# First stage of a two-block transformer kernel: which conditioning blocks are loaded and summed before the tokens are normalised

## Chip, cores and metric

The kernel runs on one core of a Trainium2 chip. The metric is the device time of one execution in microseconds; the kernel before was run three times, and it was profiled in one further execution.

## What is computed

The reference runs two transformer-like blocks on 512 tokens of width 1024, in f32. The first block starts with a conditioning step (adaptive norm), and only that and the first projection matter here:

```
c_act = silu(c)                                  # 1024 values
mod = c_act @ ada_w + ada_b                      # 6 parts of 1024: sh_t, sc_t, g_t, sh_c, sc_c, g_c
h = rms_norm(x, tm_pre_g) * (1 + sc_t) + sh_t    # 512 x 1024
p = h @ w_in                                     # all branches of the token mixer start here
```

After that come a mixer with four branches, a feed-forward network, a second block with sparse attention, and a second feed-forward network. All of them use the weights once, as they stream in.

## The kernel before

**Layout.** Activations are held transposed: 1024 channels are 8 chunks `c` of 128 partitions, with the 512 tokens along the free axis. Every f32 matrix product is made of three matmuls on split operands (`h_hi`, `h_lo` and `w_hi`, `w_lo`; lines 1244 to 1246). A weight unit `u` is 128x2048 elements, 1 MB. ScalarE copies it to `w_hi` (`split(u)`, line 716), VectorE or GpSimd makes `w_lo` from it (`lo(u)`, line 1830 or 630), and then TensorE may use it (`weights_ready(u)`). Raw weights have two buffers.

**Conditioning.** `ada_w` is 1024 x 6144. It is loaded in blocks `n` of 1 MB, 256 columns each. Blocks 0 to 7 hold the shift (`sh_t`, blocks 0 to 3) and the scale (`sc_t`, blocks 4 to 7) of the first norm. Pair `j` is the blocks `j` and `4 + j`; it belongs to the channel chunks `2j` and `2j + 1`. VectorE and TensorE share its product with `c_act`: VectorE folds six of the eight row chunks into one (`ada_sum(j)`, one instruction of line 1871 and five of line 1873), TensorE takes the other two with 16 single-column matmuls (`ada_begun(j)`, line 1385) and then adds VectorE's result with 8 more, which sum over the partitions (`ada_ended(j)`, line 1393). `ada_pair(j)` on VectorE turns the result into the shift and the gain of two chunks, and `norm_pair(j)` makes the two chunks of `h`: VectorE scales (line 1900), ScalarE makes `h_hi` (`norm_hi`, line 751), VectorE makes `h_lo` (line 1905). The scaled chunks pass through `tbuf`, which has two slots, so a pair needs the slots of the pair before it.

**Tokens.** `x` comes as four DMAs of 0.5 MB (`x_tok`, 128 tokens each). ScalarE squares and sums them, and makes 1/rms for each token. VectorE puts these on diagonals (`x_diagonal`, line 1910), and one f32 product with a matrix of ones, `ss0` (line 1410), spreads them over the partitions. TensorE transposes `x` chunk by chunk (`x_turned`, line 1336, four transposes each); ScalarE copies the chunks out (`x_copied`).

**First unit.** The weight unit `sc` is multiplied as the chunks of `h` come: `first_unit(j)` is the 12 matmuls of chunks `2j` and `2j + 1` (two output tiles of three matmuls each). Every wait stands in the order of the engine's program, and nothing overtakes it. TensorE's order before is:

```
ada_begun(0), x_turned(0..3), ada_ended(0), ss0, x_turned(4..7), weights_ready(sc),
ada_begun(1), first_unit(0), ada_ended(1), ada_begun(2), ada_ended(2), ada_begun(3),
first_unit(1), ada_ended(3), first_unit(2), first_unit(3), turn_vectors(1..5), unit sc+1, ...
```

**Queues.** SP issues the loads in one order written out by hand: blocks 0 and 4, `x`, unit `sc`, blocks 1, 5, 2, 6, then (after the last transpose of `x`, whose space they take) 3 and 7, then the next weight units as their buffers come free. GpSimd issues the constants (`cst`, the first 128 KB and the other 868 KB separately) and the small vectors, ScalarE the vectors that are needed first. After the first unit VectorE makes `lo(sc+1)`, copies the turned vectors, and the kernel goes on unit by unit.

Of the kernel before, what the change touches and what calls it, by code (L numbers as in the profile page):

```python
# [27 lines left out]
EPS = 1e-6  # L28
# [122 lines left out]
def program(nc, A, out):  # L151
# [10 lines left out]
    with ctx:  # L162
# [5 lines left out]
        def sem(name):  # L168
            if name not in sems:
                sems[name] = ctx.enter_context(nc.semaphore(name))  # L170
            return sems[name]
# [47 lines left out]
        ada_pairs = [area(at, KT, 4 * P) for at in (4864, 4864 + 2 * UNIT, 4864 + 4 * UNIT, 0)]  # L219
# [19 lines left out]
        def vector_load(eng, g):  # L239
            r = 0  # L240
            for name, n in VECTORS[g]:
                base, _, tap = name.partition("/")
                a = A[base]
                if tap:
                    src = a[0, int(tap), :].rearrange("(t p) -> t p", p=P)
                elif len(a.shape) == 3:
                    src = a[0].rearrange("k (t p) -> (k t) p", p=P)
                else:
                    src = a[0].rearrange("(t p) -> t p", p=P)
                eng.dma_start(rows_in[r:r + n, g, :], src).then_inc(sem(f"vec_in{g}"), 16)  # L250
                r += n
# [30 lines left out]
        one = small[:, 249:250]  # L282
# [5 lines left out]
        fin_s, eps = small[:, 224:236], small[:, 255:256]  # L288
# [44 lines left out]
        U, unit = {}, 0  # L333
# [140 lines left out]
        def _(sp):  # L474
# [41 lines left out]

            w, w2 = A["w_in"][0], A["w_in_2"][0]

            for n in (0, 4):
                ada_load(sp, n)  # L520
            for tt in range(TT):
                sp.dma_start(x_tok[:, tt, :], A["x"][0, tt * P:(tt + 1) * P, :]).then_inc(sem(f"x_in{tt}"), 16)

            u = U["sc"]
            cols(u, w, KT, C_SC + MIX, MIX)
            for n in (1, 5, 2, 6, 3, 7):
                if n == 3:
                    wait_full(sp, T["xT"][KT - 1])
                ada_load(sp, n)
# [81 lines left out]
        def _(pool):  # L611
            pool.dma_start(cst[:, 0:2 * P], A["consts"][:, 0:2 * P]).then_inc(sem("consts_in"), 16)
            pool.dma_start(bias_if[:, 0:1], A["ml_i_bias"].rearrange("a h -> h a")).then_inc(sem("bias_in"), 16)
            pool.dma_start(bias_if[:, 1:2], A["ml_f_bias"].rearrange("a h -> h a")).then_inc(sem("bias_in"), 16)
            pool.dma_start(gl_low[:, S:S + MIX], A["gla_w_a2"][0]).then_inc(sem("bias_in"), 16)
            for g in range(2, len(VECTORS)):
                vector_load(pool, g)
            pool.dma_start(cst[:, 2 * P:], A["consts"][:, 2 * P:N_CONST]).then_inc(sem("consts_rest"), 16)
            pool.memset(eps, EPS).then_inc(sem("eps_set"), 1)
            pool.memset(one, 1.0).then_inc(sem("eps_set"), 1)  # L620

            wait_full(pool, T["vec"][-1])
            pool.wait_ge(sem("consts_rest"), 16)
# [20 lines left out]
            for n in range(MT * TT):  # L644
                t, j = divmod(n, TT)
# [60 lines left out]
        def _(act):  # L706
# [4 lines left out]
            def split(u, i=0, units=0):  # L711

                act.wait_ge(loaded[u % 2], loaded_at(u) + (i * 16 if units else 0))
                if u >= 2:
                    act.wait_ge(w_used, u - 1 + i)
                act.activation(w_hi[u % 2][:, :], raw[u % 2][:, :], ACT.Copy).then_inc(hi_done, 1)  # L716
# [29 lines left out]
            def norm_hi(shift=None, cs=range(KT)):  # L746
                for c in cs:
                    hn[0] += 1
                    act.wait_ge(sem("h_t"), hn[0])
                    b = 0.0 if shift is None else mod[:, shift + c:shift + c + 1]  # L750
                    act.activation(h_hi[:, c, :], tbuf[:, c % 2, :], ACT.Identity, bias=b).then_inc(sem("h_hi"), 1)
# [39 lines left out]
            def x_copied(cs):  # L791
                for c in cs:
                    t = T["xT"][c]
                    wait_full(act, t)
                    act.activation(x[:, c, :], bank[t.bank][:, :], ACT.Copy).then_inc(sem("x_ready"), 1)
                    act.wait_ge(sem("x_ready"), c + 1)
                    act.nop().then_inc(read[t.bank], 1)

            x_copied(range(3))
            split(0)  # L800
            t = T["ss0"][0]
            wait_full(act, t)
            release(act.activation(rstd[:, :], bank[t.bank][:, :], ACT.Copy, scale=float(D)), t)
            x_copied(range(3, 5))
            norm_hi(0, range(2))
            x_copied(range(5, KT))
            norm_hi(0, range(2, 6))
            u = U["sc"]
            split(u + 1)
            norm_hi(0, range(6, KT))  # L810
# [426 lines left out]
        def _(pe):  # L1237
# [138 lines left out]
            def ada_begun(j):  # L1376

                t = T["ada0"][j]
                wait_free(pe, t)
                pe.wait_ge(sem("c_act"), 1)  # L1380
                for n in (j, 4 + j):
                    pe.wait_ge(sem(f"ada_in{n}"), 16)
                for at, w in ada_columns_of(j):
                    for k in range(ADA_SUMMED, KT):
                        pe.matmul(bank[t.bank][:, at:at + 1], w[:, k, :], c_act[:, k:k + 1], start=at == 0 and k == ADA_SUMMED, stop=False,
                                  skip_group_check=True)

            def ada_ended(j):

                t = T["ada0"][j]  # L1390
                pe.wait_ge(sem("ada_summed"), j + 1)
                for at, w in ada_columns_of(j):
                    mm = pe.matmul(bank[t.bank][:, at:at + 1], w[:, 0, :], one, start=False, stop=True, skip_group_check=True)
                    if at % 2:
                        mm.then_inc(sem("ada_turned"), 1)

            def x_turned(cs):
                for c in cs:
                    turn(T["xT"][c], [(tt * P, x_tok[:, tt, c * P:(c + 1) * P]) for tt in range(TT)])

            ada_begun(0)
            for tt in range(TT):
                pe.wait_ge(sem(f"x_in{tt}"), 16)
            x_turned(range(4))
            pe.wait_ge(sem("eps_set"), 2)
            ada_ended(0)
            t = T["ss0"][0]
            wait_free(pe, t)
            pe.wait_ge(sem("x_diagonal"), 1)
# [3 lines left out]
            def first_unit(j):  # L1413
                fresh_units(u, T["sc"][0:2], (2 * j, 2 * j + 1), j == 0)

            ada_begun(1)
            first_unit(0)
            ada_ended(1)
            ada_begun(2)
            ada_ended(2)  # L1420
            ada_begun(3)
            first_unit(1)
            ada_ended(3)
            first_unit(2)
            first_unit(3)
# [398 lines left out]
        def _(dve):  # L1824
            ch = Chain(dve, "dve_step")

            def lo(u, i=0):

                dve.wait_ge(hi_done, u + 1 + i)
                dve.tensor_tensor(w_lo[u % 2][:, :], raw[u % 2][:, :], w_hi[u % 2][:, :].bitcast(FP32), ALU.subtract)\  # L1830
                   .then_inc(parted[u % 2], 1)
# [62 lines left out]
            def norm_pair(j):  # L1894
# [7 lines left out]
                for c in (2 * j, 2 * j + 1):  # L1902
# [2 lines left out]
                    dve.scalar_tensor_tensor(out=h_lo[:, c, :], in0=tbuf[:, c % 2, :], scalar=mod[:, c:c + 1],  # L1905
                                             in1=h_hi[:, c, :].bitcast(FP32), op0=ALU.add, op1=ALU.subtract).then_inc(sem("h_ready"), 1)

            ada_sum(0, ada_pairs[0])
            dve.wait_ge(sem("x_rms"), 1)
            dve.tensor_tensor(tbuf[:, 0, :].rearrange("p (a b) -> p a b", a=TT), ident.unsqueeze(1).broadcast_to([P, TT, P]),  # L1910
                              rstd_tok.unsqueeze(2).broadcast_to([P, TT, P]), ALU.mult).then_inc(sem("x_diagonal"), 1)
            lo(U["sc"])
            ada_pair(0)
            wait_read(dve, T["ss0"][0])
            norm_pair(0)
            for j in range(1, 4):
                ada_sum(j, ada_pairs[j])
                if j > 1:
                    ada_pair(j - 1)
                    norm_pair(j - 1)  # L1920
            ada_pair(3)
            norm_pair(3)
            dve.wait_ge(sem("consts_rest"), 16)
            lo(U["sc"] + 1)
            for g in range(1, len(VECTORS)):
# [260 lines left out]
            for c in range(MT):  # L2186
# [17 lines left out]
                for hh in range(2):  # L2204
                    n = 2 * c + hh
# [383 lines left out]
            for c in range(4):  # L2589
                for k in range(2):  # L2590
                    t = T["wo2"][2 * c + k]
                    wait_full(dve, t)
                    n = 2 * c + k
# [18 lines left out]
            for tt in range(TT):  # L2612
                n = 2 * tt
# [41 lines left out]
```

## Time and profile before

| what | value |
|---|---|
| median of three runs | 1675.08 us (1673.26 to 1675.53) |
| the profiled execution: its own time | 1675.9 us |
| its span (first to last instruction) | 1673.7 us |
| TensorE busy | 1615.5 us, 97% of the span |
| VectorE, ScalarE, GpSimd busy | 923.5, 611.2 and 239.4 us |
| mean granted TensorE clock | 0.984 of full |
| bytes moved by DMA | 170.42 MB, 102 GB/s on average |

All times below are microseconds from the span's start. A busy time of TensorE includes matmuls that overlap in its pipeline, so the distance between starts is the better measure of a matmul.

### The profile page before, as it was taken

How to read it: one execution, taken by the hardware profiler on the slowest of the kernel's cores; microseconds unless marked ns; L12 is line 12 of the kernel's file. 1: busy time of each engine (PE TensorE's matmuls, PEld its weight loads, DVE VectorE, ACT ScalarE, POOL GpSimd, SP SyncE). 2: the span in 40 equal slices, each digit the busy share in tenths (PEclk: the TensorE clock that was granted, in tenths of full speed). 3: DMA queues.
4: the chain of work that ended last, by engine and by line, in shares of the span. 5: the costliest groups of instructions: out<-in, count | busy, mean ns of one | idle time of the engine just before them, and what ended most of it. 6: DMA issues, size and time to landing. Idle time of an engine off the chain costs nothing.

```text
span 1673.7 us, 19853 instructions
## 1 busy us (share of the span) xinstructions
PE 1615.5 (97%) x7586; PEld 1305.4 (78%) x7586; DVE 923.5 (55%) x1262; ACT 611.2 (37%) x766; POOL 239.4 (14%) x132
## 2 busy tenths in 40 slices
PE   5999999989999799999999899999999999999998
PEld 5887678768888488888888687877788888888887
DVE  5559355428786644444433667766335655556333
ACT  4333353233234443333322532343543433334223
POOL 1210024120002011101000000334342111111000
PEclk9999999989999899999999999999999999999999
DMA  9233113206763123333222234222123333332221
GB/s 334 77 101 101 51 52 100 76 26 204 227 222 101 51 76 100 100 100 100 101 92 85 74 89 134 76 76 76 51 76 101 107 86 97 100 100 100 98 92 62
DMA packets 192226, 170.42 MB, mean 102 GB/s; under 512 B 9543, under 2 KB 180900, under 8 KB 192164
## 3 DMA queue, kind: packets, MB, share of 16 engines
q1 hardware_dynamic: 174240, 150.16, 29.4%
q10 hardware_dynamic: 16948, 16.89, 3.1%
q0 software_dynamic: 976, 2.52, 0.4%
q8 instruction: 42, 0.69, 0.2%
q14 instruction: 20, 0.16, 0.0%
HBM read 165.54 MB, written 2.10 MB: 100 GB/s over the span
## 4 chain that ended last, share of the span: by engine, by line
PE 89%; DVE 6%; ACT 2%; DMA 1%; issue 1%; SPq 0%; POOL 0%; DVEq 0%; ACTq 0%
PE bank L1244 24%; PE bank L1246 23%; PE bank L1245 23%; PE bank L1251 3%; PE bank L1253 3%; PE bank L1252 3%; DVE w_lo L1830 1%; DVE work L1968 1%; PE bank L1336 1%; PE bank L1773 1%; DMA work<-in_x 1%; PE bank L1558 1%; ACT w_hi L716 1%; PE bank L1348 1%; PE bank L1758 1%
## 5 line engine op out<-in xcount | busy, mean ns | idle before, releaser
L1244 PE MATMUL bank<-h_hi,w_hi 128*128 128x512 f32 x1536 | 611.8, 398 | 12.7 <-DVE h_lo L2349 5.4
L1246 PE MATMUL bank<-h_hi,w_lo 128*128 128x512 f32 x1536 | 601.9, 392 | 0.0
L1245 PE MATMUL bank<-h_lo,w_hi 128*128 128x512 f32 x1536 | 601.2, 391 | 0.0
L1830 DVE TENSOR_TENSOR w_lo<-w_raw,w_hi 128x2048 fp32r<-128x2048 f32 x102 | 234.5, 2299 | 259.1 <-ACT w_hi L716 258.8
L1244 PEld LDWEIGHTS bank<-h_hi,w_hi 128*128 128x128 f32 x1536 | 290.5, 189 | 95.7 <-issue 27.9
L716 ACT ACTIVATE w_hi<-w_raw 128x2048 fp32r<-128x2048 f32 x131 | 250.1, 1909 | 275.1 <-PE bank L1246 170.0
L1246 PEld LDWEIGHTS bank<-h_hi,w_lo 128*128 128x128 f32 x1536 | 290.2, 189 | 62.1
L1245 PEld LDWEIGHTS bank<-h_lo,w_hi 128*128 128x128 f32 x1536 | 290.7, 189 | 59.1 <-issue 1.0
L630 POOL TENSOR_TENSOR w_lo<-w_raw,w_hi 128x2048 fp32r<-128x2048 f32 x29 | 134.3, 4630 | 545.2 <-ACT w_hi L716 545.2
L1244 PE MATMUL bank<-y_hi,w_hi 128*128 128x512 f32 x304 | 121.4, 399 | 4.9 <-DVE work L2116 3.6
L667 POOL TENSOR_TENSOR work<-work 128x512 f32 x44 | 57.0, 1296 | 458.4 <-ACT work L1044 458.4
L1246 PE MATMUL bank<-y_hi,w_lo 128*128 128x512 f32 x304 | 119.3, 392 | 0.0
L1245 PE MATMUL bank<-y_lo,w_hi 128*128 128x512 f32 x304 | 119.1, 392 | 0.0
L2318 DVE SCALAR_TENSOR_TENSOR work<-bank,par,work 128x511 f32<-128x511 f32 (+1 forms) x88 | 61.5, 743 | 77.8 <-ACT work L1038 77.8
L1038 ACT ACTIVATE work<-work,par 128x512 f32<-128x512 f32 x44 | 35.8, 815 | 106.8 <-DVE work L2307 106.8
L1244 PEld LDWEIGHTS bank<-y_hi,w_hi 128*128 128x128 f32 x304 | 57.7, 190 | 19.7 <-DVE work L2116 4.0
L1873 DVE SCALAR_TENSOR_TENSOR work<-work,small 128x256 f32<-128x256 f32 (+1 forms) x132 | 69.3, 525 | 4.7
L1251 PE MATMUL bank<-w_hi,y_hi 128*128 128x512 f32 x176 | 69.2, 393 | 0.0
L1038 ACT ACTIVATE work<-bank,par 128x512 f32<-128x512 f32 x44 | 30.0, 686 | 107.3 <-PE bank L1246 107.2
L1253 PE MATMUL bank<-w_lo,y_hi 128*128 128x512 f32 x176 | 68.5, 389 | 0.0
L1252 PE MATMUL bank<-w_hi,y_lo 128*128 128x512 f32 x176 | 68.5, 389 | 0.0
L1246 PEld LDWEIGHTS bank<-y_hi,w_lo 128*128 128x128 f32 x304 | 57.6, 189 | 12.4
(280 smaller groups left out, 1608.6 us busy)
## 6 DMA issues: line engine op xcount, KB each, us to landing
w_raw<-in_w_in SPq DMA_DIRECT2D x94, 512.0 KB, 4.7
w_raw<-in_ffn_w_up SPq DMA_DIRECT2D x44, 512.0 KB, 4.7
w_raw<-in_w_up SPq DMA_DIRECT2D x44, 512.0 KB, 5.0
work<-in_ada_w ACTq DMA_DIRECT2D x16, 1024.0 KB, 7.5
w_raw<-in_ffn_w_down SPq DMA_DIRECT2D x22, 512.0 KB, 4.0
w_raw<-in_w_down SPq DMA_DIRECT2D x22, 512.0 KB, 3.8
work<-in_ada_w SPq DMA_DIRECT2D x8, 1024.0 KB, 11.5
w_raw<-in_w_o SPq DMA_DIRECT2D x8, 512.0 KB, 4.5
```

What stands on the lines that cost most here:

```text
L630: pool.tensor_tensor(w_lo[u % 2][:, :], raw[u % 2][:, :], w_hi[u % 2][:, :].bitcast(FP32), ALU.subtract)\
L716: act.activation(w_hi[u % 2][:, :], raw[u % 2][:, :], ACT.Copy).then_inc(hi_done, 1)
L1038: act.activation(cbuf[:, k, part, :], src, ACT.Identity, scale=par[:, bass.ds(i * 2 + at, 1)], **kw).then_inc(sem("center" + n), 1)
L1244: pe.matmul(dst, w_hi[s][:, at:at + n], hi, start=first, stop=False)
L1245: pe.matmul(dst, w_hi[s][:, at:at + n], lo, start=False, stop=False)
L1246: return pe.matmul(dst, w_lo[s][:, at:at + n], hi, start=False, stop=last)
L1251: pe.matmul(dst, hi, w_hi[s][:, at:at + n], start=first, stop=False, skip_group_check=onto)
L1252: pe.matmul(dst, lo, w_hi[s][:, at:at + n], start=False, stop=False, skip_group_check=onto)
L1253: return pe.matmul(dst, hi, w_lo[s][:, at:at + n], start=False, stop=last, skip_group_check=onto)
L1830: dve.tensor_tensor(w_lo[u % 2][:, :], raw[u % 2][:, :], w_hi[u % 2][:, :].bitcast(FP32), ALU.subtract)\
L1873: ins = dve.scalar_tensor_tensor(out=unit[:, 0, :], in0=unit[:, k, :], scalar=c_act[:, k:k + 1], in1=unit[:, 0, :], op0=ALU.mult, op1=ALU.add)
L2318: ins = dve.scalar_tensor_tensor(out=c[:, back:S], in0=src[:, 0:S - back], scalar=w, in1=c[:, back:S], op0=ALU.mult, op1=ALU.add)
```

## The change

SP loads two pairs (blocks 0, 4, 1, 5) ahead of `x` instead of one. GpSimd's load of the other constants (868 KB) waits until VectorE has made `x_diagonal`, and its two small memsets move ahead of the vector loads. VectorE sums pairs 0 and 1 and finishes both before it touches the tokens, then norms both, then makes `lo(sc)`, then sums pairs 2 and 3, and only then finishes and norms these two. TensorE opens and closes both first pairs before the transposes, and multiplies the first four chunks of unit `sc` in one piece of 24 matmuls, between `ada_begun(2)` and `ada_ended(2)`. ScalarE's `split(0)` moves from ahead of the norm to between its first and second pair.

```diff
-            for n in (0, 4):
+            for n in (0, 4, 1, 5):
                 ada_load(sp, n)
             for tt in range(TT):
                 sp.dma_start(x_tok[:, tt, :], ...)
             cols(u, w, KT, C_SC + MIX, MIX)
-            for n in (1, 5, 2, 6, 3, 7):
+            for n in (2, 6, 3, 7):
...
 (GpSimd)
+            pool.memset(eps, EPS).then_inc(sem("eps_set"), 1)
+            pool.memset(one, 1.0).then_inc(sem("eps_set"), 1)
             for g in range(2, len(VECTORS)):
                 vector_load(pool, g)
+            pool.wait_ge(sem("x_diagonal"), 1)
             pool.dma_start(cst[:, 2 * P:], A["consts"][:, 2 * P:N_CONST]).then_inc(sem("consts_rest"), 16)
-            pool.memset(eps, EPS).then_inc(sem("eps_set"), 1)
-            pool.memset(one, 1.0).then_inc(sem("eps_set"), 1)
...
 (ScalarE)
             x_copied(range(3))
-            split(0)
             (rstd from ss0)
             x_copied(range(3, 5))
             norm_hi(0, range(2))
+            split(0)
+            norm_hi(0, range(2, 4))
             x_copied(range(5, KT))
-            norm_hi(0, range(2, 6))
+            norm_hi(0, range(4, 6))
             split(u + 1)
             norm_hi(0, range(6, KT))
...
 (TensorE)
+            pe.wait_ge(sem("eps_set"), 2)
             ada_begun(0)
+            ada_ended(0)
+            ada_begun(1)
+            ada_ended(1)
             (wait for the four x_in)
             x_turned(range(4))
-            pe.wait_ge(sem("eps_set"), 2)
-            ada_ended(0)
             (ss0)
             x_turned(range(4, KT))
             weights_ready(u)
-            ada_begun(1)
+            ada_begun(2)
             first_unit(0)
-            ada_ended(1)
-            ada_begun(2)
+            first_unit(1)
             ada_ended(2)
             ada_begun(3)
-            first_unit(1)
             ada_ended(3)
             first_unit(2)
             first_unit(3)
...
 (VectorE)
-            ada_sum(0, ada_pairs[0])
+            for j in range(2):
+                ada_sum(j, ada_pairs[j])
+            for j in range(2):
+                ada_pair(j)
             (wait for x_rms, x_diagonal)
-            lo(U["sc"])
-            ada_pair(0)
             wait_read(dve, T["ss0"][0])
             norm_pair(0)
-            for j in range(1, 4):
+            norm_pair(1)
+            lo(U["sc"])
+            for j in (2, 3):
                 ada_sum(j, ada_pairs[j])
-                if j > 1:
-                    ada_pair(j - 1)
-                    norm_pair(j - 1)
-            ada_pair(3)
-            norm_pair(3)
+            for j in (2, 3):
+                ada_pair(j)
+                norm_pair(j)
             dve.wait_ge(sem("consts_rest"), 16)
             lo(U["sc"] + 1)
```

## Rows read from the trace of the kernel before

**Rows 1.** The page: busy time by engine, and granted clock in 40 slices
```profile
PE 1615.5 (97%) x7586; PEld 1305.4 (78%) x7586; DVE 923.5 (55%) x1262; ACT 611.2 (37%) x766; POOL 239.4 (14%) x132
...
PEclk9999999989999899999999999999999999999999
```

**Rows 2.** Chain that ended last, 0 to 100 us: start, us, what
```profile
4.50 14.44 DMA work<-in_x
...
19.19 3.65 PE bank L1336 x16
22.84 1.50 PE bank L1393 x8
24.33 1.93 PE bank L1410 x2
26.29 0.60 ACT rstd L803
...
40.98 3.41 PE bank L1385 x16
...
46.73 0.43 PE bank L1246
...
49.12 0.79 PE bank L1393 x8
...
53.42 0.23 PE bank L1246
```

**Rows 3.** Timeline of VectorE, 0 to 75 us: start, us, line, instructions
```profile
24.72 2.29 DVE L1830 TENSOR_TENSOR w_lo<-w_raw,w_hi 128x2048 fp32r<-128x2048 f32 x1 [3.26 <-ACT w_hi L716]
...
28.98 1.41 DVE L1905 SCALAR_TENSOR_TENSOR h_lo<-tbuf,mod,h_hi 128x512 fp32r<-128x512 f32 x2 [0.25 <-ACT h_hi L751]
30.31 0.48 DVE L1871 TENSOR_SCALAR work<-work,small 128x512 f32<-128x512 f32 x1
...
34.64 0.48 DVE L1871 TENSOR_SCALAR work<-work,small 128x512 f32<-128x512 f32 x1
...
49.94 0.16 DVE L1888 TENSOR_TENSOR mod<-bank,par 128x4 f32<-128x4 f32 x1
...
53.21 2.29 DVE L1830 TENSOR_TENSOR w_lo<-w_raw,w_hi 128x2048 fp32r<-128x2048 f32 x1
```

**Rows 4.** Timeline of ScalarE, 0 to 75 us
```profile
22.78 1.91 ACT L716 ACTIVATE w_hi<-w_raw 128x2048 fp32r<-128x2048 f32 x1
...
28.22 1.33 ACT L751 ACTIVATE h_hi<-tbuf,mod 128x512 fp32r<-128x512 f32 x2
...
51.12 1.39 ACT L751 ACTIVATE h_hi<-tbuf,mod 128x512 fp32r<-128x512 f32 x2 [0.20 <-DVE tbuf L1900]
```

**Rows 5.** Timeline of TensorE, 0 to 62 us
```profile
28.65 1.84 PE L1385 MATMUL bank<-small,work 128*128 128x1 f32 x16
30.36 0.48 PE L1244 MATMUL bank<-h_hi,w_hi 128*128 128x512 f32 x1
...
55.31 0.39 PE L1246 MATMUL bank<-h_hi,w_lo 128*128 128x512 f32 x1
...
56.65 0.50 PE L1244 MATMUL bank<-h_hi,w_hi 128*128 128x512 f32 x1
```

**Rows 6.** Timeline of SP's queue: start of an issue, us
```profile
6.84 1.56 SPq L232 DMA_DIRECT2D work<-in_ada_w  x1
```

**Rows 7.** DMA issues at 6.84 and 8.5 us: KB, us to landing
```profile
work<-in_ada_w SPq DMA_DIRECT2D x1, 1024.0 KB, 18.2
...
cst<-in_consts POOLq DMA_DIRECT2D x1, 868.0 KB, 8.7
```

**Rows 8.** Windows: stretch, busy by engine, granted clock, DMA share, GB/s
```profile
27.80:38.00 10.20, 8.41 (x61) 7.46 (x59) 9.63 (x15) 3.30 (x6) 0.00 (x0) 1.00 1.09 348
38.00:48.30 10.30, 9.19 (x34) 8.32 (x35) 9.82 (x18) 1.95 (x3) 0.00 (x0) 0.50 0.71 226
...
362.30:365.70 3.40, 3.40 (x10) 2.51 (x9) 0.74 (x1) 0.00 (x0) 0.00 (x0) 0.50 0.00 0
```

## The prediction

> **What bounds the kernel now.** I read the page first: TensorE is busy 97% of the span [rows 1], so after the opening the time is TensorE's own work, and a change in the opening is worth exactly what it moves the moment from which TensorE is fed without a break. I take two marks for this moment: the end of the 48 matmuls of unit `sc` at 55.70, and the start of unit `sc+1` at 56.65 [rows 5]. Later weights have no fixed date: each load waits for a buffer that the work itself frees, so what is gained or lost at 56.65 should be kept to the end, one for one.
>
> Then I read the chain of waits for the opening. It has three parts. Until 18.94 it is the landing of the tokens. From 19.19 to 26.89 it is TensorE with 16 transposes, the closing of pair 0 (1.50) and `ss0` (1.93), then ScalarE's `rstd` (0.60) [rows 2]. From there VectorE has work without a pause: two normed chunks until 30.39, and then the sums of pairs 1, 2 and 3, at 34.64 - 30.31 = 4.33 each, with the norms between them, until `lo(sc+1)` starts at 53.21 [rows 3]. TensorE follows it.
>
> Last I read the clock. It is granted in full from 27.8 to 38.0 and at one half (1.2 of 2.4 GHz) from 38.0 to 48.3 [rows 8]. Ahead of that fall TensorE had only single-column matmuls and pauses since 33.2, where its first 12 full matmuls ended (30.36 + 12 x 0.23); the clock came back after some 4 us of full matmuls, which began at 44.4 (40.98 + 3.41) [rows 2, 5]. A full matmul starts every 0.43 at half clock and every 0.23 at full clock; opening a pair takes 3.5 against 1.84, closing one took 1.50 before the tokens' end and 0.79 at full clock [rows 2, 5].
>
> **The change, step by step.** All times are on the axis of the profile before.
>
> *Tokens land.* In SP's order before, block 1 is the sixth MB, and it landed at 6.84 + 18.2 = 25.0 [rows 6, 7]. The tokens now end with the sixth MB. The 868 KB of constants shared the engines until 8.5 + 8.7 = 17.2 [rows 7] and no longer do: 0.89 MB at the 348 GB/s of a full queue [rows 8] is 2.55. Tokens: 25.0 - 2.55 = 22.5. If moving the constants were worth nothing it would be 25.0, the upper bound. The landing of the constants itself is hidden: they are first needed after the first unit, past 53. Behind the tokens the queue then brings unit `sc` (3.0 for a MB, 25.5), blocks 2 and 6 and the constants (34.1), and blocks 3 and 7, which SP issues after the last transpose, at 32 (40.1); their sum starts at 42.4, so this is hidden with 2.3 to spare.
>
> The row shows a transfer from GpSimd's queue landing while SP's stream is running [rows 7]. The Trainium skill, DMA: Bandwidth & Descriptors, "Issuing engines are not separate DMA queues", says that transfers of all issuing engines interleave on the same 16 DMA engines. By that rule the removed 868 KB is worth its full share; were the two queues apart, it would be worth nothing, and the tokens would land at 25.0.
>
> *Pair 1 before the tokens.* Block 5 is now the fourth MB; the fourth MB landed at 18.94 [rows 2], less 2.55 it is 16.4. Sum 1 ends 4.33 later, at 20.8, or 21.3 if the last half MB lags. TensorE closes pair 1 in 1.50, so it is free at 22.3 to 22.8. That is the same moment as the landing of the tokens; I take 22.8 as the start of the transposes, against 19.19: **+3.6**. Pair 0 is closed earlier, in idle time: **-1.5**. So `rstd` is ready at 22.8 + 3.65 + 1.93 + 0.60 = 29.0, against 26.89: **+2.1**. These 2.1 are the price for one sum of 4.33 taken off VectorE's later work.
>
> *First two pairs normed.* Pair 0 takes what it took before, 26.89 to 30.39 [rows 3]: 32.5. Pair 1: VectorE scales both chunks by 33.9. ScalarE has ended `h_hi` 1 at 29.55 + 2.1 = 31.65, but now makes `split(0)`, 1.91, first, then two `h_hi` in 1.33 [rows 4], until 35.0. The last `h_lo` ends at 35.8. Then comes `lo(sc)`, 2.29 [rows 3]: 38.1. Before, the split and `lo(sc)` lay in VectorE's and ScalarE's waiting time for `ss0`, and cost nothing. Now they stand in the row: `weights_ready(sc)` opens at 38.1 instead of before 30, so the first matmul of the unit, at 30.36 before [rows 5], has to come after 38.1, and so does `ada_begun(2)`, which stands behind that wait though it needs no weights.
>
> *TensorE from 38.1.* It has been idle since about 32, where its last 16 transposes end (28.4 + 3.65). That is a longer pause than the one before 38.0, so I take half clock: opening pair 2 takes 3.5, to 41.6. Then 24 matmuls: as before, the first 4 us (9 matmuls) at half clock and the other 15 at 0.23, together 7.5, until 49.1. Closing pair 2 takes 0.8: 49.9. Opening and closing pair 3 take 1.84 + 0.79: 52.5. VectorE has summed pairs 2 and 3 in the meantime (38.1 + 2 x 4.33 = 46.8) and waits 3.1 for the closing of pair 2. This is a new wait: TensorE, not VectorE, sets the middle now. Behind it on VectorE stand everything of pairs 2 and 3 and `lo(sc+1)`.
>
> *Last two pairs.* Finishing and norming a pair takes 53.21 - 49.94 = 3.3 [rows 3]: pair 2 is ready at 49.9 + 3.3 = 53.2, its first chunk at 52.5, when TensorE is free too. Pair 3 starts at 53.2. ScalarE puts `split(sc+1)` between them: `h_hi` 5 ends 2.6 after the parameters (51.12 + 1.39 against 49.94 [rows 3, 4]), so 52.5; the split ends at 54.4, `h_hi` 6 and 7 at 55.9, where they would without it be at 55.8; it is hidden. Chunk 6 is ready at 55.9, chunk 7 at 56.6. TensorE has done chunks 4 and 5 (12 x 0.23) by 55.4, waits 0.5, and ends at 55.9 + 2.8 + 0.15 = **58.85**, against 55.70: **+3.15**. `lo(sc+1)` ends at 58.9, as close to TensorE's end as before, so unit `sc+1` moves by the same: from 56.65 to 59.8.
>
> *The sum.* From the end of pair 0's `h_lo`, now at 32.5: 3.3 for pair 1 with the split in it, 2.3 for `lo(sc)`, 11.8 for TensorE's opening, 24 matmuls and closing, 6.0 until chunk 6 is ready, 2.95 for the last 12 matmuls: 26.35. Before, from 30.39: three sums (13.0) and three norms (9.8) to 53.21, and TensorE 2.5 more: 25.3. The difference is +1.05, and with the +2.1 of `rstd` it is +3.15. The profiled execution took 1675.9 with a span of 1673.7; the changed one would take 1679.1. The median of the runs is 0.8 below the profiled one: 1675.1 + 3.1 = **1678.2**.
>
> *What costs nothing.* The two memsets move a few instructions earlier on GpSimd and `one` is needed only at the first closing, at about 15. GpSimd's new wait for `x_diagonal` has behind it the constants and then pads and weight parts that belong to units after the first; the small vectors stand ahead of it. SP issues the same loads in number; `sc+2`, whose buffer `lo(sc)` frees, can now start at 38.1 only and lands in the forties, and it is wanted after `sc+1` has begun, past 56.65.
>
> *Bounds of the unsure terms.* Half clock during the 24 matmuls can last from 2 us to all of them: 0.2 us lost per 0.43 us, so -0.9 to +2.8 on the sum. If the clock falls once more while pair 3 is opened and closed (3.4 us without a full matmul), a stretch such as those found later, 3.4 us long [rows 8], costs half its length, +1.7. Tokens at 25.0 instead of 22.5: +2.2. Sum 1 without the lag: -0.5.
>
> **Rivals.**
>
> *R1: full clock; VectorE sets the end.* If TensorE ran at full clock from 38.1, it would have closed pair 2 at 38.1 + 1.84 + 5.6 + 0.8 = 46.3, before VectorE ends the sums at 46.8. Then pair 3 is normed at 46.8 + 6.6 = 53.4, and TensorE ends at 55.7: **0.0**, 1675.1. For it: the 24 matmuls are now one piece, where 12 stood between waits. Against it: the wait ahead of them is 6 us, and the clock fell after less [rows 2, 8]. It decides the time if half clock, which costs the forecast 1.7 in the opening and 1.9 in the matmuls, is absent from both; with it in one of them alone the sum is about +1.4. On this the Trainium skill, TensorE: Matmul & The Clock Gate, "Loop structure matters more than you think", says that matmuls back to back keep the clock full and that a long wait between them drops it; its first half speaks for R1, its second for the forecast, and the fall in [rows 8] agrees with the second.
>
> *R2: more half clock.* The fall during pair 3's opening comes, or the first recovery takes nearly the whole piece: **+4.6 to +6**, 1680 to 1681. For it: before, 4.8 us without full matmuls brought the fall at 38.0. Against it: here it is only 3.4.
>
> *R3: the constants' move is worth nothing,* or moving block 1 delays the tokens by more: tokens at 25.0, **+5.3**, 1680.4. Against it: the queue is full, at 348 GB/s, in the whole stretch [rows 8].
>
> *R4, the other sign: later half-clock stretches.* The page shows slices below 9 or at 8 later [rows 1], and such a stretch costs TensorE half of its 3.4 us [rows 8]. Everything after the opening starts at another moment, so some of these stretches may not come. Each of 3.4 us that is gone gives 1.7; two turn +3.1 into **-0.3**, 1674.8, and four are needed to be faster by over 0.2%. Against it: the pauses that bring them are those of the program, and the three runs lie within 2.3.
>
> **How the numbers follow.** The forecast, +2.2 to +4.6, has 0.55; R1 and what lies between it and the forecast 0.16; R2 0.17; R3 0.06; R4 0.06. What a measurement of this kernel can tell from no change is about 0.2%, 3.35 us, and the forecast lies just inside it. Faster by more: 0.03 of R4, and 0.01 for all else. Within: 0.32 of the forecast, 0.16 of R1, 0.03 of R4. Slower by more: 0.23 of the forecast, and R2 and R3. That is 0.04, 0.51 and 0.45. The range goes from R1 less half a microsecond of scatter, 1674.6, to R2 with half a microsecond, 1681.8.
>
> **What the profile of the changed kernel would show.** Tokens landing at 22 to 23; transposes from 22.8; `rstd` at 29.0; `lo(sc)` ending at about 38.1, with TensorE idle for some 6 us ahead of it; a clock of 0.50 when `ada_begun(2)` starts; VectorE waiting about 3 us for `ada_ended(2)`; unit `sc` ending near 58.9 and `sc+1` starting near 59.8. The distance between this start and the end of the span should be the 1617 us of before. The prediction is wrong if TensorE comes back at full clock, if VectorE doesn't wait for pair 2, or if that last distance changes.

## The result, and the profile after

| | before | changed |
|---|---|---|
| median | 1675.23 us (14 runs, 1673.26 to 1676.31) | 1679.34 us (14 runs, 1678.07 to 1681.00) |
| ratio | | 1.0024, 95% interval 1.0017 to 1.0032 |
| profiled execution: span | 1673.7 us | 1678.2 us |
| start of unit `sc+1` | 56.65 | 61.10 |
| from there to the end of the span | 1617.05 | 1617.10 |

The change costs 4.1 us. The forecast was +3.1, 1678.2, with a range of 1674.6 to 1681.8; the time is inside it, 1.1 above the value. It lies just above the 0.2% (3.35 us) of the prediction, on the side that had a chance of 0.45; the interval of the ratio, 0.17% to 0.32%, excludes "no change" but reaches to both sides of that 0.2%.

The page of the changed kernel, busy times and granted clock:

```profile
PE 1617.6 (96%) x7586; PEld 1307.6 (78%) x7586; DVE 924.0 (55%) x1262; ACT 611.3 (36%) x766; POOL 239.5 (14%) x132
...
PEclk9999999989999899999999999999999999999999
```

No engine has more instructions than in [rows 1]; TensorE's busy time is 2.1 longer with the same number of matmuls. The 4.5 us of span are idle time and slower matmuls, and the table says where: in this pair of profiles all of it lies ahead of `sc+1`. The chain of the changed kernel that ended last, in its first 100 us (start, us, what):

```profile
3.49 13.94 DMA work<-in_ada_w
17.53 0.50 DVE work L1873
...
22.01 1.87 PE bank L1395 x8
23.87 3.52 PE bank L1338 x16
27.39 1.62 PE bank L1414 x2
29.03 0.60 ACT rstd L803
...
32.30 1.80 ACT w_hi L717
...
36.16 2.21 DVE w_lo L1832
38.42 3.58 PE bank L1387 x16
...
49.42 0.79 PE bank L1395 x8
50.20 1.79 PE bank L1387 x16
51.99 0.99 PE bank L1395 x8
```

Against [rows 2], the chain no longer starts with the tokens but with block 5 (lands at 17.4), VectorE's sum of pair 1 and its closing (line 1395, `ada_ended`). `rstd` ends at 29.63, 2.7 later than before. Then two steps stand in the chain that were not in it: `split(0)` (line 717) and `lo(sc)` (line 1832). The opening of pair 2 (line 1387) comes directly behind the latter.

VectorE's timeline in the changed kernel:

```profile
36.08 2.29 DVE L1832 TENSOR_TENSOR w_lo<-w_raw,w_hi 128x2048 fp32r<-128x2048 f32 x1
...
43.13 3.90 DVE L1875 SCALAR_TENSOR_TENSOR work<-work,small 128x512 f32<-128x512 f32 x5
50.24 0.16 DVE L1890 TENSOR_TENSOR mod<-bank,par 128x4 f32<-128x4 f32 x1 [3.21 <-PE bank L1395]
...
56.77 2.29 DVE L1832 TENSOR_TENSOR w_lo<-w_raw,w_hi 128x2048 fp32r<-128x2048 f32 x1
```

In [rows 3] VectorE had no pause above 0.25 from `rstd` to 53.21. Here its sums are done at 47.03 and it waits 3.21 us for TensorE to close pair 2. And TensorE, in windows (busy by engine, granted clock, DMA):

```profile
28.80:35.60 6.80, 1.94 (x17) 1.67 (x15) 5.01 (x8) 6.31 (x9) 0.00 (x0) 1.00 1.05 363
35.60:45.80 10.20, 7.38 (x25) 6.56 (x26) 9.88 (x13) 1.40 (x3) 0.00 (x0) 0.50 0.95 305
45.80:52.70 6.90, 6.90 (x48) 6.26 (x46) 3.46 (x7) 1.28 (x2) 0.00 (x0) 0.99 0.00 0
52.70:56.10 3.40, 3.40 (x9) 2.67 (x9) 3.20 (x7) 3.29 (x4) 0.00 (x0) 0.50 0.01 2
```

As in [rows 8] there is one long stretch at half clock (1.2 of 2.4 GHz). The clock fell during the idle time ahead of 38.4. The second one, 52.7 to 56.1, meets the first of the last 24 matmuls; ahead of it lie 3.5 us in which TensorE had only single-column matmuls.

### The profile page after: what moved, and what is told of

The parts are those of the page before. It is cut to its first block, busy times and chain, and to the rows that moved or that the text cites. A ratio compares the mean times of both kernels' runs of the same rounds, so it can differ in the third digit from the quotient of the medians.

```text
span 1678.2 us, 19854 instructions
## 1 busy us (share of the span) xinstructions
PE 1617.6 (96%) x7586; PEld 1307.6 (78%) x7586; DVE 924.0 (55%) x1262; ACT 611.3 (36%) x766; POOL 239.5 (14%) x132
## 4 chain that ended last, share of the span: by engine, by line
PE 89%; DVE 6%; ACT 2%; DMA 1%; issue 1%; SPq 0%; POOL 0%; DVEq 0%; ACTq 0%
PE bank L1246 24%; PE bank L1248 23%; PE bank L1247 23%; PE bank L1253 3%; PE bank L1254 3%; PE bank L1255 3%; DVE w_lo L1832 1%; DVE work L1971 1%; PE bank L1338 1%; PE bank L1775 1%; DMA work<-in_ada_w 1%; PE bank L1560 1%; ACT w_hi L717 1%; PE bank L1350 1%; PE bank L1760 1%
## 5 line engine op out<-in xcount | busy, mean ns | idle before, releaser
L2321 DVE SCALAR_TENSOR_TENSOR work<-work,par 128x511 f32<-128x511 f32 (+1 forms) x88 | 61.9, 746 | 9.6 <-ACT work L1040 9.6
```

The costliest lines, as they stand in the source:

```text
L2321: ins = dve.scalar_tensor_tensor(out=c[:, back:S], in0=src[:, 0:S - back], scalar=w, in1=c[:, back:S], op0=ALU.mult, op1=ALU.add)
```

## Experiments

All times of marks are from each run's own profile, on its own axis. "Tail" is the span less the start of `sc+1`. Ratios are against the runs of the kernel before on the same chip.

| run | median us | ratio (95%) | pair 0's norm starts | `sc+1` starts | tail |
|---|---|---|---|---|---|
| changed kernel | 1679.34 | 1.0024 (1.0017 to 1.0032) | 29.66 | 61.10 | 1617.1 |
| 1. opening of pair 2 early | 1677.43 | 1.0008 (0.9998 to 1.0017) | 30.32 | 58.41 | 1617.0 |
| 2. split and `lo(sc)` early | 1676.11 | 1.0006 (0.9996 to 1.0016) | 31.89 | 58.51 | 1616.3 |
| 3. before, constants late | 1674.03 | 0.9992 (0.9982 to 1.0002) | 25.46 | 57.60 | 1615.4 |
| 4. changed, constants early | 1682.57 | 1.0039 (1.0025 to 1.0053) | 32.06 | 64.75 | 1615.1 |
| 5. changed, kept busy | 1677.06 | 1.0011 (1.0001 to 1.0020) | 30.25 | 61.64 | 1615.3 |
| 6. `lo(sc)` early, kept busy | 1674.00 | 0.9993 (0.9983 to 1.0002) | 31.73 | 57.19 | 1613.9 |
| 7. before, constants last | 1673.48 | 0.9986 (0.9977 to 0.9996) | 25.70 | 55.59 | 1615.9 |
| 8. the same, five row chunks | 1675.68 | 1.0001 (0.9992 to 1.0011) | 25.08 | 57.02 | 1616.7 |
| 9. opening early, kept busy | 1677.27 | 1.0014 (1.0004 to 1.0023) | 29.14 | 57.56 | 1617.4 |
| 10. all hidden, kept busy | 1677.37 | 1.0013 (1.0004 to 1.0022) | 30.48 | 57.92 | 1617.2 |
| 11. all hidden | 1674.73 | 0.9999 (0.9990 to 1.0008) | 30.78 | 56.56 | 1616.9 |
| 12. before, constants last, kept busy | 1673.46 | 0.9992 (0.9983 to 1.0001) | 25.21 | 54.43 | 1614.1 |

In the kernel before, pair 0's norm starts at 27.32 and `sc+1` at 56.65. The tail was expected to be constant. With the kernel before there are fourteen profiles; it is 1616.9 to 1617.4 in six of them and up to 3.2 us shorter in others. So the time of a whole run can't decide a question of one microsecond here, and the start of `sc+1` is the measure below. Each start is from one profile, though, and part of what moves it lies ahead of most of the edits: `ss0` alone took from 0.9 to 1.9 us in these profiles. So where an edit stands behind the norm, the distance between the last two starts is the safer measure.

**1. The opening of pair 2 ahead of the wait for weights.**

```diff
             x_turned(range(4, KT))
+            ada_begun(2)
             weights_ready(u)
-            ada_begun(2)
             first_unit(0)
             first_unit(1)
```

> The changed kernel, with the opening of pair 2 (ada_begun(2)) ahead of TensorE's wait for the weights of unit sc. Theory A (TensorE sets the middle, because the opening stands behind a wait that it does not need): the opening runs at about 33.7 to 37.2, once block 6 has landed; the 24 matmuls start at 38.3 instead of 42.0, and VectorE's wait for the closing of pair 2 (3.2 us) disappears, since the sums end at 47.0. Unit sc+1 starts about 3 us earlier than in the changed kernel (61.1), at about 58; the time is 3 us below the changed kernel's. Rival B (the half clock is the cause and not the order): the clock falls as before, the matmuls take what they took, and the start of sc+1 moves by less than 1.5 us. Rival C (only the later tokens cost): no change.

Measured: `sc+1` at 58.41, 2.7 earlier. TensorE and VectorE in that run:

```profile
34.43 1.92 PE L1387 MATMUL bank<-small,work 128*128 128x1 f32 x16 [3.03 <-DMA work<-in_ada_w]
```

```profile
47.59 0.16 DVE L1890 TENSOR_TENSOR mod<-bank,par 128x4 f32<-128x4 f32 x1
```

The opening waits for block 6 and then runs in the idle time; VectorE passes from its sums to pair 2 without a wait. The 24 matmuls still started at half clock (39.1 to 46.7). Theory A holds, B and C don't: the new order alone removes the loss in the middle, and half clock in the 24 matmuls costs nothing once VectorE's sums cover it. Whether full clock in the old order would have removed it too is not shown: 1.7 us of the 3.58 that the opening took there were half clock, and the run that was to tell, run 5, lost its clock.

**2. Split and `lo(sc)` back in the wait for `ss0`.**

```diff
 (ScalarE)
             x_copied(range(3))
+            split(0)
             (rstd from ss0)
             x_copied(range(3, 5))
-            norm_hi(0, range(2))
-            split(0)
-            norm_hi(0, range(2, 4))
+            norm_hi(0, range(4))
 (VectorE, behind x_diagonal)
+            lo(U["sc"])
             norm_pair(0)
             norm_pair(1)
-            lo(U["sc"])
```

> The changed kernel, with split(0) and lo(sc) put back into the wait for ss0, as before; everything else as changed. Theory A: lo(sc) ends at about 29.3, before rstd (29.6), and is hidden again. h_lo of pair 1 ends at about 36.0 with no lo behind it, the sums of pairs 2 and 3 end at 44.6, TensorE opens pair 2 when block 6 has landed (33.7) and has the 24 matmuls, the closing and pair 3 done by about 46.4. VectorE sets the end. Unit sc+1 starts at about 54.5, which is 6.6 us below the changed kernel and 2 us below the kernel before. Rival B (half clock): the 24 matmuls still run half at half clock and sc+1 starts no more than 3 us earlier. Rival C (only the later tokens cost): no change against the changed kernel.

Measured: `sc+1` at 58.51, 2.6 earlier and not 6.6. The expectation was wrong in two places. ScalarE's split stands behind the three copies of `x`, which now come one by one behind the late transposes, so `lo(sc)` starts at 29.7 and is hidden only in part; pair 0's norm has to wait for its end, 31.89:

```profile
29.68 2.29 DVE L1831 TENSOR_TENSOR w_lo<-w_raw,w_hi 128x2048 fp32r<-128x2048 f32 x1 [4.08 <-ACT w_hi L717]
```

And half clock met both pieces of the unit (windows of this run):

```profile
34.50:41.30 6.80, 6.80 (x25) 6.03 (x25) 6.50 (x11) 3.06 (x5) 0.00 (x0) 0.50 1.09 350
...
48.20:55.00 6.80, 6.43 (x17) 5.09 (x17) 6.58 (x9) 3.84 (x4) 0.00 (x0) 0.50 0.00 1
```

The last 24 matmuls took from 49.03 to 57.4, 8.4 where they take 5.6 at full clock. VectorE had finished `lo(sc+1)` at 55.1 and waited for TensorE.

**3 and 4. The constants alone.** First in the kernel before, then taken out of the changed one:

```diff
 (GpSimd, before + this)
+            pool.memset(eps, EPS).then_inc(sem("eps_set"), 1)
+            pool.memset(one, 1.0).then_inc(sem("eps_set"), 1)
             for g in range(2, len(VECTORS)):
                 vector_load(pool, g)
+            pool.wait_ge(sem("x_diagonal"), 1)
             pool.dma_start(cst[:, 2 * P:], ...)
-            pool.memset(eps, EPS).then_inc(sem("eps_set"), 1)
-            pool.memset(one, 1.0).then_inc(sem("eps_set"), 1)
 (GpSimd, changed kernel)
-            pool.wait_ge(sem("x_diagonal"), 1)
```

> The kernel before, with one part of the change alone: the 868 KB of constants wait for x_diagonal, and the two memsets come first. Theory A (the transfers share one stream): tokens land 2.5 us earlier, at 16.4, rstd is ready at 24.4 instead of 26.9, and as VectorE is busy without a pause from there, sc+1 starts 2.5 us earlier, at 54.2; time 2.5 us below the kernel before (1672.7). Rival (the queues do not take from each other, or something else sets the start): no change.

> The changed kernel without its wait for x_diagonal on GpSimd: the constants load early again. Theory A: blocks 1 and 5 and the tokens land about 2.5 us later than in the changed kernel (block 5 at 20, tokens at 25.0), and all that follows with them: sc+1 starts at 63.6, time 2.5 us above the changed kernel, 1681.8. Rival (constants cost nothing): no change.

In the kernel before, the transposes start at 17.30 instead of 19.19, but `sc+1` at 57.60 instead of 56.65. VectorE's timeline shows why:

```profile
34.30 0.49 DVE L1872 TENSOR_SCALAR work<-work,small 128x512 f32<-128x512 f32 x1 [1.45 <-DMA work<-in_ada_w]
```

The constants now share the engines with blocks 2 and 6, and the sum of pair 2 waits for them; TensorE then waits 1.28 for block 7 as well. That 1.28 is passed on: opening, 12 matmuls and closing of pair 3 then run at half clock or behind it, and VectorE waits 1.27 for that closing. The gain of 1.9 at the tokens was given back at the later blocks. In the changed kernel the removed wait moves the transposes from 23.73 to 26.73 and `sc+1` to 64.75, 3.65 later: the constants' new place was worth 3.0 at the tokens there. The rest lies in the last 24 matmuls, which met more half clock and took 8.4 instead of 7.0, less 0.6 that a faster `ss0` gave back.

**5 and 6. TensorE kept busy in the pauses.** `keep_busy(n)` runs `n` extra f32 matmuls of 128x256 on constants into bank 7; no result uses them.

```diff
+            def keep_busy(n):
+                wait_read(pe, T["ss0"][0])
+                for _ in range(n):
+                    pe.matmul(bank[7][:, 0:2 * P], const("ones_d"), cst[:, 0:2 * P], start=True, stop=True)
 (run 5, on the changed kernel)
             x_turned(range(4, KT))
+            keep_busy(15)
             weights_ready(u)
 (run 6, on run 2: keep_busy(8) there, and)
             ada_begun(3)
+            keep_busy(4)
             ada_ended(3)
```

> The changed kernel with 15 extra f32 matmuls (128x256, constants into a bank that is free) on TensorE in the idle time ahead of the wait for the weights of unit sc; their result is used by nothing. Theory A (the late start of the unit costs as forecast, and half clock adds 3.1 by making TensorE set the middle): the extra matmuls run at full clock from 30.7 to 37.3, the opening of pair 2 takes 1.8 instead of 3.5, the 24 matmuls 5.6 instead of 7.4, VectorE's wait for pair 2 goes from 3.2 to 0, sc+1 starts at 56.9 instead of 61.1 (58.2 if the clock falls in the gap ahead of the last 24 matmuls). Rival C (the later tokens are the cause, TensorE is not): sc+1 moves by less than 1. Rival D (such filler does not hold the clock): opening still 3.5 and sc+1 later than 61.1.

> The lo-early version of the changed kernel with 8 such extra matmuls ahead of the wait for the weights and 4 between the opening and the closing of pair 3. It is to tell why the lo-early version started sc+1 at 58.5 and not at the 54.5 expected. Theory A (two half-clock stretches, 34.5 to 41.3 and 48.2 to 55.0, took 3 us, the rest is lo(sc), which ended at 31.9, 2.3 after rstd, and was only half hidden): with full clock throughout, sc+1 starts at 56.1, VectorE setting the end. Rival (something else holds TensorE, such as the landing of block 6 at 34.3): sc+1 stays above 57.5 although the clock is full.

Run 5 did not do what it was made for. The extra matmuls ran at full clock until 38.0; after 1.07 us of pause, and in the middle of the 16 single-column matmuls of the opening, the clock fell all the same (at 40.0), before the unit:

```profile
31.31 6.64 PE L1406 MATMUL bank<-cst 128*128 128x256 f32 x30
39.02 2.73 PE L1387 MATMUL bank<-small,work 128*128 128x1 f32 x16 [1.07 <-DVE w_lo L1838]
```

```profile
40.00:46.80 6.80, 6.80 (x21) 5.71 (x21) 6.51 (x10) 0.00 (x0) 0.00 (x0) 0.50 0.83 264
```

`sc+1` started at 61.64, as far behind pair 0's norm as in the changed kernel (31.4 in both). Run 6 has full clock until 45.6 and the 24 matmuls in 5.7 us, so closing pair 2 waits only for VectorE's sum; but half clock from 45.6 to 52.4 stretched the filler, the closing of pair 3 and the last piece (48.87 to 56.09). `sc+1` at 57.19, 1.3 before run 2, 1.1 behind its expectation.

**7 and 8. The kernel before with the constants last; and with five row chunks on VectorE.**

```diff
 (run 7: as run 3, but)
-            pool.wait_ge(sem("x_diagonal"), 1)
+            pool.wait_ge(sem("ada_in7"), 16)
 (run 8: run 7 and)
-ADA_SUMMED = 6
+ADA_SUMMED = 5
```

> The kernel before, with the 868 KB of constants waiting for block 7 of the conditioning weights instead of for x_diagonal, and the two memsets first. Theory A (every MB ahead of the tokens costs them 3 us, and in the earlier run the constants only moved their cost from the tokens to blocks 2 and 6): tokens 1.9 to 2.5 earlier than before, block 6 no later than before, no wait of VectorE for a block, sc+1 at 54.3 to 54.8 against 56.65, time 2 us below the kernel before. Rival (sc+1 is set by TensorE's half clock and not by the tokens): sc+1 no earlier than 56.

> The same as the run with the constants last, and VectorE folds five row chunks of a conditioning pair instead of six; TensorE takes three (24 single-column matmuls for an opening instead of 16). Theory A (from rstd on VectorE sets the pace, and TensorE has some room): each sum takes 3.6 instead of 4.3, an opening 0.9 more at full and 1.8 more at half clock; sc+1 starts 1 us earlier than with the constants last alone, at about 53.5. Rival (TensorE is already as tight as VectorE): no gain, or up to 2 us later.

Run 7: the transposes start 1.6 us earlier (17.57), and pair 0's norm with them (25.70; `rstd` was ready at 23.56, but `lo(sc)` ended only at 25.3); no sum waits for a block, and `sc+1` starts at 55.59, 1.1 earlier than before. It was expected 1 us earlier still. Its chain has TensorE in it where VectorE was expected: it waits for block 7 (by 0.19), then opens pair 3 at half clock, and VectorE waits 0.71 for the closing:

```profile
26.45 12.34 DMA work<-in_ada_w
38.92 3.54 PE bank L1386 x16
```

Run 8 makes each sum 0.79 shorter and TensorE's openings longer (24 single-column matmuls, 5.26 at half clock), and `sc+1` comes at 57.02. VectorE waits for the closing of pair 3:

```profile
50.31 0.16 DVE L1889 TENSOR_TENSOR mod<-bank,par 128x4 f32<-128x4 f32 x1 [4.60 <-PE bank L1394]
```

In the opening of this kernel, with its half clock, TensorE is as tight as VectorE, and taking a part of each sum from VectorE is worth nothing by itself.

**9. The opening early, and every pause filled.** Run 1 with `keep_busy(8)` before and `keep_busy(5)` after `ada_begun(2)`, `keep_busy(2)` before and `keep_busy(3)` after `ada_ended(3)`.

> The changed kernel with the opening of pair 2 early (as in the first run) and extra f32 matmuls, used by nothing, in every pause of TensorE: 8 before and 5 after that opening, 2 before and 3 after the closing of pair 3. With the opening out of the way there is no run of single-column matmuls right ahead of the unit, which is where the clock fell in the run that was kept busy. Theory A (half clock costs what it takes from the last 24 matmuls, 1.4 us, and VectorE sets the rest): full clock from 31 on, sc+1 at 57.3, against 58.4 with the early opening alone. Rival D (filler does not hold the clock): sc+1 at 58.4 or later.

Half clock was left in 48.0 to 51.4 only. The last piece runs from 50.29 to 56.46, 6.2 instead of 7.0; `sc+1` at 57.56, 0.85 earlier than run 1, with 1.1 expected. Its first chunk was ready at 49.1, but the last `keep_busy(3)` ran at half clock, 2.91, and held the piece back by 1.2. And the 0.85 is not the filler's: pair 0's norm began 1.2 earlier than in run 1, ahead of all filler, because the transposes began 0.4 earlier and `ss0` took 0.9 instead of 1.7:

```profile
29.14 1.41 DVE L1911 SCALAR_TENSOR_TENSOR tbuf<-x,gain,rstd 128x512 f32<-128x512 f32 x2 [3.75 <-ACT rstd L803]
```

Counted from that norm `sc+1` came 0.3 later than in run 1 (28.4 against 28.1). The filler gained nothing, and Theory A of this run is not borne out.

**10 and 11. The priced losses taken out, with and without filler.**

```diff
 (run 11: run 2, and on ScalarE)
+            split(0)
             x_copied(range(3))
-            split(0)
 (GpSimd)
-            pool.wait_ge(sem("x_diagonal"), 1)
+            pool.wait_ge(sem("ada_in7"), 16)
 (run 10: also keep_busy(2) ahead of weights_ready(u),
  keep_busy(3) before and keep_busy(4) after ada_ended(3))
```

> The changed kernel with all of its priced losses removed: split(0) ahead of the copies of x and lo(sc) in the wait for ss0, the constants after block 7, and a few extra f32 matmuls in TensorE's pauses. Theory A (the losses are those places and not the two pairs ahead of the tokens): lo(sc) ends by 29.3 and rstd comes at 29.6; the four chunks of h are ready at 36.0, the sums end at 44.7, VectorE sets the end, sc+1 starts at 54.6, 2 us ahead of the kernel before and 6.5 ahead of the changed one. Rival C (the later tokens outweigh the sum taken off VectorE): sc+1 at 56.6 or later even so.

> The same without the extra matmuls. Theory A: half clock returns in both stretches; in the first it is covered by VectorE's sums, in the last 24 matmuls it costs 1.4 to 2.8: sc+1 at 56 to 57. Rival (the clock does not matter once the order is right): the same start as with the extra matmuls, 54.6.

Run 11: `sc+1` at 56.56, within its expectation of 56 to 57, and equal to the kernel before, 56.65. But one loss stayed. `split(0)` now waits for the landing of unit `sc` with the copies of `x` and `rstd` behind it:

```profile
26.20 1.91 ACT L717 ACTIVATE w_hi<-w_raw 128x2048 fp32r<-128x2048 f32 x1 [1.23 <-DMA w_raw<-in_w_in]
28.01 2.01 ACT L796 ACTIVATE x<-bank 128x512 f32<-128x512 f32 x3
30.15 0.60 ACT L804 ACTIVATE rstd<-bank 128x512 f32<-128x512 f32 x1
```

`rstd` came 6.5 after the start of the transposes, where it came after 5.1 in run 9 with an equally fast `ss0`, and at 30.75 instead of the 29.6 expected; `lo(sc)` ended at 30.4 and not by 29.3. So about 1.3 us of the split is still in the row. Run 10, with filler, was 1.4 later, not 2 earlier: the filler itself ran at half clock and held the last piece back.

```profile
47.28 3.76 PE L1405 MATMUL bank<-cst 128*128 128x256 f32 x8
```

VectorE had the first chunk ready at 48.1; the piece began at 50.48. So run 10 does not decide between its theories, and with the split in the way run 11 doesn't either.

**12. Run 7 with filler** (`keep_busy` of 4, 3, 3, 2 and 4 ahead of `ada_begun(1)`, after `first_unit(0)`, before `ada_ended(2)`, and before and after `ada_ended(3)`).

> The kernel before with the constants last, and extra f32 matmuls in TensorE's pauses (4, 3, 3, 2 and 4). Theory A (there the start of sc+1 at 55.6 was late by half clock in the opening of pair 3 and in the first matmuls behind it): sc+1 at 54.8, VectorE without a wait. Rival D (filler does not hold the clock, or delays what stands behind it): sc+1 at 55.6 or later.

Full clock throughout, and the earliest start of all, 54.43 against 54.8 expected:

```profile
27.80:54.40 26.60, 26.10 (x153) 22.31 (x151) 24.97 (x42) 8.74 (x13) 0.57 (x1) 1.00 0.70 227
```

The opening is 2.2 us faster than before; 2.1 of that is there at pair 0's norm already. Counted from that norm, full clock brings 0.7 against run 7 (29.2 against 29.9). Its times scatter more than those of run 7 (1670.65 to 1676.54 against 1671.34 to 1673.91), and the interval of its ratio contains 1. Run 7 is the version to keep: 0.9986, 0.9977 to 0.9996, with one added wait and no filler. Its interval lies below 1, but the gain is less than 0.2%, and 1.2 of its profile's 2.2 us come from a shorter tail; the earlier start of `sc+1`, 1.1, is the part that is explained.

## Why the prediction was right, step by step

The direction, the mechanism and the places were right, and one term that the forecast put at nothing, a second fall of the clock, came. The terms:

| step | predicted | measured |
|---|---|---|
| start of the transposes | 22.8 | 23.87 |
| `rstd` ready | 29.0 | 29.63 |
| `lo(sc)` ends | 38.1 | 38.37 |
| 24 matmuls begin, end | 41.6, 49.1 | 42.0, 49.4 |
| VectorE's wait for pair 2 | 3.1 | 3.21 |
| pair 2's parameters start | 49.9 | 50.24 |
| last piece begins | 52.5 | 52.98 |
| unit `sc` ends | 58.85 | 60.15 |
| `sc+1` starts | 59.8 | 61.10 |

**Tokens and pair 1.** Block 5 landed at 17.4, not at 16.4 or 17, and closing pair 1 took 1.87 instead of 1.50, so TensorE's start was late by 1.07. I had taken 1.50 from the closing in the kernel before, which was part of a run of matmuls that went on. `ss0` at the later date was faster, 1.62 against 1.93. Together +0.6 on `rstd`: the +2.1 was +2.7. Runs 4, 3 and 7 show that the stream is shared: the constants' place moved the transposes by 3.0 in the changed kernel and 1.6 to 1.9 in the one before, with 2.5 expected in both. R3 was wrong: the move of the constants was worth its price.

**Split and `lo(sc)` in the row.** 38.37 against 38.1. The runs show that this costs: from the start of the transposes to the start of sum 2 it is 14.55 us in the changed kernel, 13.45 with them moved back in part (run 2), and 12.76 in run 11. Of these differences, 0.7 to 0.8 are the faster `ss0` of the two runs.

**The opening behind the wait.** Run 1 measures it: `sc+1` comes 2.7 earlier, or 3.3 counted from the start of the transposes, which was 0.6 later in that run. That is the 3.2 that VectorE waited. It is the biggest single term, though order and half clock share in it.

**Clock.** The fall ahead of 38.4 came as forecast, and its length, some 4 us into the full matmuls, too (41.9 to 45.8). The other fall, R2's, which had a chance inside 0.17, came as well: the last piece took 7.0 instead of 5.6. This term was left out of the forecast with the argument that 3.4 us without a full matmul is less than the 4.8 before. That argument failed: the fall came at 52.7, 3.3 after the last full matmul had ended. In runs 1, 2, 4, 5 and 11 the last piece met half clock too. It is the step that was mis-sized: the piece was 1.4 slower, of which 0.5 took the place of the wait for chunk 6 that the forecast had, so 0 predicted and some +0.8 measured; with the 0.5 from the steps ahead this is the 1.3 by which the two marks came late. That the total still came within 1.1 is because the term was small, not because it was foreseen. In run 9, with less half clock, the piece was 0.8 shorter.

**R1.** The Trainium skill, TensorE: Matmul & The Clock Gate, "Loop structure matters more than you think", says that a long wait between matmuls drops the clock, and the trace agrees (0.50 from 35.6, in an idle time of 7.68 us). The fall in [rows 8], which the prediction took for the same, is not so clear a case: the pauses ahead of it were of 1.41 and 1.49 us only. Run 5 was to price R1 and could not, since the clock fell. Run 1 bounds it instead: with the opening out of the way, half clock in the 24 matmuls is covered by VectorE's sums. What full clock would have been worth in the order of the changed kernel stays open.

**R4.** The tail of the changed kernel's profile is the same as before, 1617.1 against 1617.05, and so are its later stretches at half clock: eight in both, each about 4.5 us later. But the idea had something in it: in six of the other profiles it was 1.2 to 3.2 shorter. I gave it 0.06, and it is about as large as many effects looked for here. That the tail did not move in this pair is in part luck.

**One for one.** In the profiles the loss of 4.45 at `sc+1` is the loss of 4.5 in the span. The medians give 4.1: the device time lies 2.2 above the span in the profiled execution before and 1.9 above it in the changed one, and what makes that difference was not looked for.

**Where the idea's gain went.** A sum of 4.33 was taken off VectorE after `rstd`. It was paid with 2.7 for `rstd`, since 2 MB more stand ahead of the tokens and TensorE closes pair 1 first; 1.6 is left. Run 11 ties with the kernel before at `sc+1`, but that doesn't weigh the two orders against each other: about 1.3 us of the split are still in its row, its last 24 matmuls took 7.0 with half clock, and its constants come last, which is worth 1.1 in the old order (run 7, 55.59, is 1.0 ahead of it). Whether two pairs ahead of the tokens can win with all of this settled is open.

## What to carry to other kernels

In an in-order engine, look at what stands behind a wait that it does not need: one block of small matmuls behind `weights_ready` was the largest part of this loss, and moving one line took it away. What is hidden in a wait, such as a split ahead of a norm, costs its length when it has to stand elsewhere in the row. When a transfer is moved out of the way of one consumer, follow it to the next: the constants had to go behind the last block, not just behind the tokens, before the kernel gained.

## What the runs showed of the hardware that was not expected

In run 5 TensorE's clock fell within the 16 single-column matmuls of an opening. They followed 6.64 us of full matmuls and a pause of 1.07, and the clock was at 0.50 from 40.0 on. At the start, transposes and the f32 `ss0` were what came before the rise: in the kernel before, 16 single-column matmuls took 3.54 us at 10.63 and 1.84 at 28.65. The views show 1.00 for the first of these too, so ahead of the first recorded change the clock is better read from durations.

Filler matmuls are not free: `keep_busy(8)` took 3.62 at full clock in run 6 (16 records, two for each f32 matmul), so 4 take 1.8; in run 10 `keep_busy(4)` took 3.76 at half clock, and the work behind it was late by 2.4.

The time from a fixed point of the program to its end, with the same instructions behind it, was between 1613.9 and 1617.4 us in fourteen profiles. Windows around one of the later stretches show that the clock there differs between profiles; in the kernel before, and in run 12:

```profile
225.00:245.00 20.00, 16.44 (x66) 12.12 (x66) 15.62 (x21) 7.26 (x10) 4.25 (x2) 0.91 0.17 54
```

```profile
225.00:245.00 20.00, 16.43 (x67) 12.13 (x66) 14.07 (x23) 8.83 (x12) 5.67 (x2) 1.00 0.17 53
```

About the same work at the same busy time (66 and 67 matmuls), with a stretch at half clock in the first and none in the second. Run 6, the other one with a short tail (1613.9), has none there either. But the mean clock doesn't order the tails: it is 0.982 with 1615.9 in run 7 and 0.985 with 1617.4 in run 9. What decides it was not tested.
